# The buffers of SBUF laid out anew: weights at 0 modulo 1024 bytes, the high part of the input at -128, the low part at -192, the arena at -256

## The reference

```
# first block, twice
x = x + 0.5 * swiglu(rms_norm(x, ffn1_norm), w_gate, w_up, w_down)      # 1024 -> 2816 -> 1024
h = rms_norm(x, mix_norm);  a, g, q, k, v = split(h @ w_in)
x = x + concat(conv_module(a, g), diff_attention(q, k, v)) @ w_out      # conv of 31 taps, 4 heads
x = x + 0.5 * swiglu(rms_norm(x, ffn2_norm), ...)
# second block: layer 0 retention, layer 1 gated spatial unit, each followed by peer_ffn
mod = silu(c) @ ada_w + ada_b                                            # shifts, scales, gates
x = x + g1 * retention_mixer(h)      /  sgu_mixer(h)
q = h @ w_query; top 16 of 128 keys twice, 8 heads; best 16 of 256 sums; softmax -> gates
x = x + g2 * sum over the chosen of 16384 experts: gelu(h . u_e) * gate_e * v_e
```

## Time and profile before

| | |
|---|---|
| median of three runs | 3594.24 us |
| the profiled execution's own time | 3592.3 us |
| its span, first to last instruction | 3590.0 us |
| TensorE (PE) busy | 3340.8 us, 93% |
| VectorE (DVE) / ScalarE (ACT) / GpSimd (POOL) busy | 2223.3 / 1669.9 / 358.7 us |
| granted TensorE clock, mean | 0.928 of full |
| HBM traffic | 181 GB/s over the span |

### The profile page before, as it was taken

How to read it: one execution, slowest core, us unless ns; L and a number is a source line. 1 busy time by engine, 2 the same in 40 slices (tenths; PEclk the granted TensorE clock), 3 DMA queues, 4 the chain that set the end, 5 groups by cost and what they waited for, 6 DMA issues and landing times.

```text
span 3590.0 us, 53567 instructions
## 1 busy us (share of the span) xinstructions
PE 3340.8 (93%) x22596; PEld 3053.5 (85%) x22596; DVE 2223.3 (62%) x3486; ACT 1669.9 (47%) x2436; POOL 358.7 (10%) x313
## 2 busy tenths in 40 slices
PE   7996799997699999969999999999998899999999
PEld 7995799996599999967789999878998678999987
DVE  5766586866477655775445555666658554555566
ACT  5445454544455445533344444556444233444454
POOL 0015000005100001740000000000066000000000
PEclk9998899998799999986799999999999678999999
DMA  6661276664057544433376666654444336666663
GB/s 224 231 220 61 98 254 223 247 236 143 21 199 257 176 165 160 149 127 129 141 234 211 212 215 217 225 193 176 153 154 152 117 129 223 213 215 215 216 233 129
DMA packets 153262, 654.62 MB, mean 182 GB/s; under 512 B 10332, under 2 KB 77472, under 8 KB 78272
## 3 DMA queue, kind: packets, MB, share of 16 engines
q1 hardware_dynamic: 80064, 575.70, 45.3%
q10 hardware_dynamic: 72544, 74.05, 6.3%
q0 software_dynamic: 416, 1.45, 0.2%
HBM read 616.55 MB, written 34.61 MB: 181 GB/s over the span
## 4 chain that ended last, share of the span: by engine, by line
PE 88%; DVE 6%; ACT 4%; issue 1%; ACTq 1%; DMA 0%; DVEq 0%
PE ps L567 19%; PE ps L568 19%; PE ps L569 19%; PE ps L898 7%; PE ps L572 6%; PE ps L573 6%; PE ps L574 6%; PE ps L693 2%; DVE w_lo L1359 1%; PE ps L617 1%; ACT w_hi L967 1%; ACTq L1268 1%; PE ps L872 0%; DVE at L1547 0%; DVE at L1813 0%
## 5 line engine op out<-in xcount | busy, mean ns | idle before, releaser
L1359 DVE TENSOR_TENSOR w_lo<-raw,w_hi 128x1024 fp32r<-128x1024 f32 x912 | 1115.9, 1228 | 739.8 <-ACT w_hi L967 738.9
L967 ACT ACTIVATE w_hi<-raw 128x1024 fp32r<-128x1024 f32 x1000 | 1053.0, 1056 | 924.0 <-PE ps L569 684.3
L567 PE MATMUL ps<-h_hi,w_hi 128*128 128x256 f32 x4416 | 1275.6, 289 | 49.9 <-DVE w_lo L1359 41.9
L568 PE MATMUL ps<-h_lo,w_hi 128*128 128x256 f32 x4416 | 1259.6, 285 | 0.0
L569 PE MATMUL ps<-h_hi,w_lo 128*128 128x256 f32 x4416 | 1257.7, 285 | 0.0
L567 PEld LDWEIGHTS ps<-h_hi,w_hi 128*128 128x128 f32 x4416 | 864.0, 196 | 62.9 <-issue 38.0
L568 PEld LDWEIGHTS ps<-h_lo,w_hi 128*128 128x128 f32 x4416 | 865.3, 196 | 3.7 <-issue 0.2
L569 PEld LDWEIGHTS ps<-h_hi,w_lo 128*128 128x128 f32 x4416 | 866.8, 196 | 0.0
L572 PE MATMUL ps<-w_hi,at 128*128 128x512 f32 x1024 | 398.5, 389 | 3.1 <-DVE at L1862 3.1
L574 PE MATMUL ps<-w_hi,at 128*128 128x512 f32 x1024 | 398.4, 389 | 0.0
L573 PE MATMUL ps<-w_lo,at 128*128 128x512 f32 x1024 | 398.3, 389 | 0.0
(11 more groups left out here) (256 smaller groups left out, 3039.6 us busy)
## 6 DMA issues: line engine op xcount, KB each, us to landing
raw<-in_peer_u SPq DMA_DIRECT2D x128, 1024.0 KB, 4.8
raw<-in_peer_v SPq DMA_DIRECT2D x128, 1024.0 KB, 4.8
raw<-in_ffn_gu SPq DMA_DIRECT2D x88, 1024.0 KB, 4.9
raw<-in_ada_w SPq DMA_DIRECT2D x48, 1024.0 KB, 4.9
raw<-in_ffn_down SPq DMA_DIRECT2D x44, 1024.0 KB, 5.0
gates<-at ACTq DMA_DIRECT2D x32, 1024.0 KB, 4.3
at<-gates ACTq DMA_DIRECT2D x32, 1024.0 KB, 6.1
raw<-in_w_in SPq DMA_DIRECT2D x16, 1024.0 KB, 4.8
```

The costliest lines, as they stand in the source:

```text
L567: e.matmul(o, lhs[0], rhs[0], start=start, stop=False)
L568: e.matmul(o, lhs[0], rhs[1], start=False, stop=False)
L967: e.activation(whi[:, u % NPAIR, :], raw(k, half), ACT.Copy).then_inc(hi_done.hit(u), 1)
L1359: e.tensor_tensor(wlo[:, m % NPAIR, :], raw(k, half), whi[:, m % NPAIR, :].bitcast(FP), ALU.subtract).then_inc(w_lo_dve.hit(m), 1)
```

## The change: the diff and where each buffer starts

The change alters addresses alone. On all five engines the instructions, their order and their waits are word for word those of before; only the line numbers of the source move, by 11 (12 behind the `carve` line).

```diff
-        x = sb("x", [128, KT, T])
-        hh_ = sb("h_hi", [128, KT, T], FR)
-        hl_ = sb("h_lo", [128, KT, T], FR)
-        sq = sb("sq", [128, 2, T])
-        tmp_h = sb("tmp_h", [128, 3, T])
+        def begin(name, residue):
+            at = (nc.sbuf_base + 31) // 32 * 32
+            if (residue - at) % 1024:
+                sb(name, [128, (residue - at) % 1024], mybir.dt.uint8)
+
+        cols = sb("cols", [128, NCOL])
         ident = sb("ident", [128, 128])
         ones = sb("ones", [128, 128])
+        begin("gap0", 896)
+        hh_ = sb("h_hi", [128, KT, T], FR)
+        iota = sb("iota", [128, 128], HF)
         half1 = sb("half1", [128, 128])
-        iota = sb("iota", [128, 128], HF)
+        begin("gap1", 832)
+        hl_ = sb("h_lo", [128, KT, T], FR)
+        begin("gap2", 0)
+        whi = sb("w_hi", [128, NPAIR, UNIT], FR)
+        wlo = sb("w_lo", [128, NPAIR, UNIT], FR)
+        raw_t = sb("raw", [128, NRAW, 2 * UNIT])
+        x = sb("x", [128, KT, T])
...
-        raw_t = sb("raw", [128, NRAW, 2 * UNIT])
-        whi = sb("w_hi", [128, NPAIR, UNIT], FR)
-        wlo = sb("w_lo", [128, NPAIR, UNIT], FR)
+        begin("gap3", 768)
         NA = 29000
...
         sb("arena", [128, NA])
+        sq = sb("sq", [128, 2, T])
+        tmp_h = sb("tmp_h", [128, 3, T])
+        rr = sb("rr", [128, T])
...
         mdiag = [carve(128) for _ in range(4)]
+        carve, end = carver(place, -(-end[0] // T) * T)
         cat_hi, cat_lo = carve(8, T, dt=FR), carve(8, T, dt=FR)
```

More of the change, by code:

```diff
@@ L170, in signal @@
             return Signal(ctx.enter_context(nc.semaphore(name)), order)
-        x = sb("x", [128, KT, T])
-        hh_ = sb("h_hi", [128, KT, T], FR)
-        hl_ = sb("h_lo", [128, KT, T], FR)
-        sq = sb("sq", [128, 2, T])
-        tmp_h = sb("tmp_h", [128, 3, T])
+        def begin(name, residue):
[3 more added lines that the diff above has]
+        cols = sb("cols", [128, NCOL])
         ident = sb("ident", [128, 128])
         ones = sb("ones", [128, 128])
+        begin("gap0", 896)
+        hh_ = sb("h_hi", [128, KT, T], FR)
+        iota = sb("iota", [128, 128], HF)
         half1 = sb("half1", [128, 128])
-        iota = sb("iota", [128, 128], HF)
+        begin("gap1", 832)
[5 more added lines that the diff above has]
+        x = sb("x", [128, KT, T])
         iota16 = sb("iota16", [128, 16], HF)
-        cols = sb("cols", [128, NCOL])
         epsc = sb("epsc", [128, 2])
-        rr = sb("rr", [128, T])
         rcol = sb("rcol", [128, 2])
-        rdiag = tmp_h[:, 2, :].rearrange("p (a b) -> p a b", a=2)
         mod = sb("mod", [128, L, 48])
@@ L190, in build @@
         subg = sb("subg", [128, L])
-        raw_t = sb("raw", [128, NRAW, 2 * UNIT])
-        whi = sb("w_hi", [128, NPAIR, UNIT], FR)
-        wlo = sb("w_lo", [128, NPAIR, UNIT], FR)
+        begin("gap3", 768)
         NA = 29000
         arena_at = (nc.sbuf_base + 31) // 32 * 32
+        assert arena_at % 1024 == 768, arena_at % 1024
         sb("arena", [128, NA])
+        sq = sb("sq", [128, 2, T])
+        tmp_h = sb("tmp_h", [128, 3, T])
+        rr = sb("rr", [128, T])
+        rdiag = tmp_h[:, 2, :].rearrange("p (a b) -> p a b", a=2)
         def place(at, *shape, dt=FP):
```

## The result

The changed kernel takes 3611.56 us, median of six runs (3607.32 to 3612.86), against 3593.88 us before (3593.0 to 3597.89): ratio 1.0044, 95% interval 1.0031 to 1.0057, some 18 us more where 124 less were forecast. The profiled execution took 3612.45 us, 20 us over the one of before.

What follows compares the result with a forecast made beforehand. PE's step from matmul to matmul was taken as the bound. Gains summed to 125.6 us, less 2 for small waits: 3592.3 - 124 = 3468.3 for the profiled execution, so 3470 us as median, range 3438 to 3545.

Steps and rivals of the forecast that it cites:

- The excess comes from two reads side by side and depends on where they lie: 256-column steps exceed 107 ns by 6 to 13 without waits, ordered by distance between the two SBUF reads.
- It falls as the loaded operand lies further ahead: Excess shrinks from -64 over 0 and 32 to 64 bytes; the change takes every distance to between 128 and 384.
- The 20.7 us for the 7400 matmuls at 113: Gain on `h` matmuls in the faster pattern, steps from 113.3 to 110.5 ns.
- The 36.0 us for the 5000 at 118: Gain on `h` matmuls in the slower pattern, mostly between expert sums, steps from 117.7 to 110.5 ns.
- The arena's 31.1 us: Gain on arena pairs: 28.2 us for 2970 at full clock, 120 to 110.5 ns, plus 2.9 us for `cat`.
- the expert sum's 33.8 us: Gain on 3072 matmuls of 512 columns, durations from 389 to 378 ns.
- `project_rows` was 0 for 4: Gain of 4 us, half of 7.5, on 576 matmuls going from 391 to 378 ns.
- The floor of 110.5: Step taken for 256 columns after the change, from float32 matmuls of 128 columns with steps of 111 to 112 ns.
- Only part of it goes: Rival: 113 is a floor of the load-and-stream pair; gain of 63 us, 3531 us; chance 0.20.
- The rival that repeats every 256 bytes: Arena and expert sum unchanged (sign: arena stays 283), `h` mean 118.3, 40 us more, 3634; chance 0.10, a part 0.02.
- the taps' 377/378 against 379/381: Evidence against the 256-byte rival: conv taps at distances 160 to 344 had 377/378, L721 at 0 had 379/381.
- The two patterns of one distance: `h` at one distance runs at 276 or 281 ns; 5000 put at 281; after the change they should be one.

Runs made afterwards that it cites:

- map1: Kernel of matmuls alone, 256-column fp32r triples, inputs at chosen distances to the weights; steps of 113.3 ns at 64 bytes, 120.0 at 0 and 256.
- h64: The changed kernel with only h_hi and h_lo moved back to distance 64 from the weights; 3595.9 us, ratio 1.0007 to the kernel before.
- map3: Matmuls alone: grid of w_lo and lo places, various widths, and a still stream (one moving float repeated), 111.7 ns at distances 0, 64 and 128.
- all64: The changed kernel with h_hi, h_lo and the whole arena at distance 64 from the weights; 3575.66 us (0.9952), in another session 3569.97 us (0.9919).
- map4: Matmuls alone: 12 wide matmuls, a filler, then 96 of 256 columns at distance 64 or 128; at 64, 113.3 or 117.8 ns depending on the filler.

## Why the prediction was wrong, point by point

**What bounds the kernel: right.** PE's step sets the time; no DMA, DVE or ACT wait changed by more than a few microseconds.

**The excess comes from two reads side by side and depends on where they lie: right.** map1, h64 and the still stream of map3 show it.

**"It falls as the loaded operand lies further ahead": this is the step that failed.** The points at 0, 32 and 64 bytes (steps of 120, 118 and 113 ns), with the wide matmuls' 391 at -64 against 389 at 0, were extended to 128 and beyond as a slope. They were samples of a jagged pattern: 64 is one of two good places in 256 bytes, its neighbours 56 and 72 have 120. The change moved `h` off the one good place it had, by chance, before: (64, 64) with 113.3 or 117.8 became (128, 192) with 117 to 119. With it every term of the sum failed. The 20.7 us for the 7400 matmuls at 113 became a loss of about 33, since their steps went up to 117 or 119. The 36.0 us for the 5000 at 118 were 2 us in the expert stage. The arena's 31.1 us and the expert sum's 33.8 us were 0, as 256 is the same place as 0. `project_rows` was 0 for 4.

**The floor of 110.5 was too low, and its row was misread.** The still stream has 111.7 and the best pair found 113.3. Of the 1.6 ns between them no experiment says whether it can be avoided. The row with 128 columns of plain float32 shows no load alone: by the earlier trace rows 256 such columns have a step of 215 ns and 128 have 111, so 128 of them stream for some 104 ns, as long as 256 of fp32r and not half as long. That map3 found 111.7 close to it is luck. For 512 columns a plain float32 matmul of 256 columns was the wrong neighbour: it streams half as many bytes in a nanosecond. At 512 columns the best place measured pays 13.3 ns over the columns, which is the 389 that was there.

**"Only part of it goes".** Its 113 as a floor of the pair agrees with all maps, in which no walking stream of 256 columns is under 113.3; its 63 us did not come, since no step moved to that floor.

**The rival that repeats every 256 bytes: right in mechanism, size half, and its prices by luck.** It said arena and expert sum unchanged (283 and 389: so they are; 283 was its own sign), `h` up to 118.3 (117.7 measured), 40 us more. Its mean came close because two wrong prices offset each other: 115 at distance 128 and 125 at 192, where map1 has 118.7 and 117.8, and 117.0 for the pair. It had 0.10 and 0.02 for a part of it, since the taps' 377/378 against 379/381 was taken as evidence against. That was a difference of 2 ns in another kind of matmul, laid against a question that rows of the same kind could not answer; with no fp32r row beyond distance 64, two periods were open, and the ends of the sum should have been +40 and -124 with similar weight. Its size was off because the mean rose by 2.5 ns and not by 3.2, which makes 31 us of the 40, and because 11 of the 31 did not show in the time: 7 are idle time that PE lost, 4 were not found.

**The two patterns of one distance** were seen and counted about rightly (5000 and 7400; a mean of 115.2 between 113.3 and 117.8 gives some 5200 of 12,360), but "one floor for both" was assumed. They are two stable ways for one pair of places, and the entry decides.

**The pages.** The still stream's 111.7 against 113 to 121 with a walking one, and the 6.7 ns between distance 0 and 64, contradict the sentence of the Trainium skill ("TensorE: Matmul & The Clock Gate", Part 2) by which loading the next weights takes nothing from the running matmul. Its gap of columns / 2.4 + 2.5 ns ("Back-to-back issue gap"), which it calls that of an isolated matmul, was reached by no fp32r step here: 113.3 at the best where it gives 109.2, 226.7 where it gives 215.8.

## The version that beats both

all64 is 0.5 to 0.8% faster than the kernel before (0.9952, 0.9919 in two sessions) and 0.9 to 1.2% faster than the change, by the ratios to the kernel before. Its gain comes by putting each streaming input 64 bytes below the weights instead of 128 to 256. In its profile the arena steps fell from 119.8 to 113.7 in the mean, which is 20 us for some 3270 of them, and the two expert sums took 7 less. Single executions lay between 3558 and 3584 us, about as far apart as those of the kernel before beside them (3587 to 3607). At least a part of that is the pattern that each `h` stage falls into, 4.5 us a stage (above); what decides it in a given execution was not tested.

## What to carry to other kernels

Where fp32r matmuls of 256 columns run back to back with a weight load each, the start addresses of the streaming and the loaded operand are worth up to 8 ns in 113, for nothing but a gap in the allocation; but the map is jagged and 256 bytes further nearly the same, so measure it with a kernel of matmuls alone, in one run of a millisecond, and do not reason along a slope. Before trusting three or four points of an address effect, ask at which period they would look the same. And a change of layout for one kind of product must be priced for each kind that shares the buffers, and for the entry from one kind into the next.

## What the runs showed of the hardware that was not expected

- Steps of fp32r matmuls of 256 columns at full clock have recurring sizes (113.3, 117.0, 117.8, 118.7, 120.0 ns are the commonest) that depend on the operands' starts; for equal distances they were the same 256 bytes further in all eight cases of map1, for unequal ones not always.
- The same instructions at the same addresses have two stable steps, 113.3 and 117.8, and three small matmuls at the entry are enough to go from one to the other (map4). Two executions of one kernel had them the other way round in the same stage.
- At distance 0 wide matmuls cost 13.3 ns over their columns at 320, 384 and 512 columns and 16 at 448; at 128 and 192 columns the distances 0, 64 and 128 made no difference.
- Which places of `w_lo` against `w_hi` and of `lo` against `hi` are good beyond the measured grid, and what in SBUF makes 64 and 144 good, stays open.
